# Token-major projection blocks as quads of 256 x 512 weight tiles in a hybrid decoder layer

## The chip, the cores and the metric

The kernel runs on one core of a Trainium2 chip. The metric is the device time of one execution in microseconds (us). Times of single instructions come from one profiled execution.

## What is computed

One decoder layer for 512 tokens of width 1024, batch 1, in float32. The normalised input goes through one combined projection, whose columns feed two mixers and two gates:

```python
h = rms_norm(x, norm1_w)
(q, k_c, v_c, k_s, v_s, k_w, v_w, g_nsa, z, xbc, dt_raw, gate_a, gate_b) = split_columns(h @ w_in, IN_SIZES)
y_a = nsa_mixer(...)      # 16 heads in 4 groups: compressed, selected and sliding-window attention
y_b = ssd_mixer(...)      # Mamba-2 scan, 32 heads in 4 groups, gated by silu(z), normalised per group
merged = sigmoid(gate_a) * (y_a @ w_proj_a) + sigmoid(gate_b) * (y_b @ w_proj_b)
x = x + merged @ w_out
x = x + conv_glu_ffn(rms_norm(x, norm2_w), ...)
```

## The kernel before, in words

**Split numbers.** Each product is made from three matmuls: high by high, high by low, low by high. A weight unit of 1024 x 128 is loaded by SyncE into one of two buffers `wraw` (two DMAs of 256 KB). ScalarE rounds it into `w_high` (`hi`, L1022, the activation is L1027), VectorE subtracts that and writes `w_low` (`lo`, L1548, the instruction L1551). Both have four slots. `load` for unit u waits until `lo(u - 2)` is done; `hi(u)` waits until TensorE is done with what lay in the slot. The activations lie transposed in `hT`, high and low.

**Phases.** 13 blocks come first (projections for the compressor and for group 0), then four groups g = 0 to 3 of 14 blocks each, then gates, the merge, the output projection and the feed-forward network. A block is one weight unit. The blocks of a group are OB, OC, then eight that are called windows n = 0 to 7 here, then four OX. Windows 0 to 3 (OQ) make queries, keys and values of the next group (in group 3: four gate blocks), windows 4 to 7 (OZ) make z of this group.

**Forms of a block.** `block_of` (through `gemm` and `ktile`, L609 to L611) holds a weight tile in the array and moves 512 tokens. `half_pair` (L637, matmuls L650 to L652) is token-major: it holds 128 x 128 tokens and moves the 256 columns of two neighbouring units; a pair of units takes two half_pairs, each of two token tiles, and each fills one of the two block banks `gb` (48 matmuls of 256 columns). It waits for both units of its pair.

**The interleave.** Every engine runs a list written out by hand. TensorE has eight places in a window, each of six matmuls of 256 columns (or three of 512). Between them it does, in window n: the scores of attention unit n + 1 (ahead of place 0), the weighted values of unit n - 1 (place 1), and the transposes of unit n's probabilities, j = 0, 1 at place 3 and j = 2, 3 at place 6 (window 0: places 2 and 5; window 7: 5 and 7). In window 0 of groups 1 to 3 the last y transposes stand at place 0. The transposes use two banks `tb` in turn, and each waits for the release (`t_rel`) of the one two before.

ScalarE, in stage n: `pT_hi` for j = 0, 1 (L1331), the exponentials of unit n + 1 for tiles 3 and 2 (L1294), `pT_hi` for j = 2, 3, the exponentials for tiles 1 and 0, the first convolution tap (L1101), and `evac_mid` (L1224), which copies the finished block out of its bank (for heads also a square for the norm) and ends with `hi(u + 3)`. In groups 1 to 3 it comes to stage 0 from `y_back_out` (L1183): four copies of y transposes into `ystage` (piece_e, L1189), each releasing a `tb` bank. `evac_x(g, 5)` (L1087), the evacuation of block OC with `hi` of unit OQ + 2, stands in stage 0 after the second `pT_hi`.

VectorE, in stage n:

```python
scale(n)                                  # L1835 to L1841, releases p_ready for the transposes of unit n
if n < 7: ttr(n + 1)                      # L1782, reads the scores, frees their banks
if n in (2, 4, 6): out_fold(n // 2 - 1)
lo(u0 + 4 + n)                            # unit OQ + 2 + n
p_low(n, ...)                             # L1853, releases the tb banks
if n > 1: conv(g, CONVS[n - 2])           # L1601
```

In stage 0 `comp_exponents` and `comp_probs`, in stage 1 `cmp_low`, in 5 `k_sums` and in 7 `q_sums` come besides. GpSimd does little in these windows.

## Time and profile before

| what | us |
|---|---|
| runs | 1243.45, 1243.58, 1244.14 |
| median | 1243.58 |
| profiled execution, span from first to last instruction | 1241.6 |
| TensorE busy | 1229.4 |
| VectorE busy | 843.6 |
| ScalarE busy | 635.3 |
| eight windows of group 1 (263.6 to 337.5) | 73.9 |

The span is from the first to the last instruction of the profiled execution. The profile gives no separate time for what lies outside the span; the median of the runs is 2.0 us above it. A matmul's length in the trace is modelled and overlaps the next one, so that the distance between starts tells what one costs. In a timeline row the columns are start, length, engine, line, operation, output<-inputs, shapes, count, and in brackets the idle time before it with its releaser.

### The profile page before, as it was taken

What the parts mean: (1) busy time and instruction counts of PE and PEld (TensorE: products, weight loads), DVE (VectorE), ACT (ScalarE), POOL (GpSimd) and SP (SyncE); (2) the same over time, 40 slices, a digit from 0 to 9 for tenths busy, and PEclk for the clock granted to TensorE, in tenths of its full rate; (3) what the DMA queues carried; (4) which work ended last, traced back from release to release, by engine and by line L of the source; (5) the groups of instructions that cost most, each with busy time, mean ns of one, the idle gap of its engine ahead of it and who ended that gap; (6) DMA issues with size and microseconds to landing.
All of it is one profiled execution on the core that took longest, in us unless ns stands there. A gap on an engine that the chain in (4) does not pass through costs nothing.

```text
span 1241.6 us, 17772 instructions
## 1 busy us (share of the span) xinstructions
PE 1229.4 (99%) x6725; PEld 1054.2 (85%) x6725; DVE 843.6 (68%) x1611; ACT 635.3 (51%) x1201; POOL 88.3 (7%) x78
## 2 busy tenths in 40 slices
PE   7999999999999999999999999999999999999998
PEld 6998998899978998888978888888888888888887
DVE  4526988898879887899774643333788888884221
ACT  6616777678775868676775633223423222332110
POOL 1000001400042001400040000000000000000000
PEclk9999999999999999999999999999999999999999
DMA  8512321132212221132116623335233333334341
GB/s 243 162 34 66 86 60 47 48 105 63 63 44 74 80 67 54 51 102 61 54 40 219 222 86 93 93 97 179 64 102 96 91 102 102 88 101 136 102 128 42
DMA packets 185737, 116.34 MB, mean 94 GB/s; under 512 B 25933, under 2 KB 169909, under 8 KB 185653
## 3 DMA queue, kind: packets, MB, share of 16 engines
q1 hardware_dynamic: 182023, 108.86, 30.5%
q10 hardware_dynamic: 3630, 6.35, 1.4%
q8 instruction: 54, 0.88, 0.3%
q14 instruction: 30, 0.25, 0.1%
HBM read 106.80 MB, written 8.39 MB: 93 GB/s over the span
## 4 chain that ended last, share of the span: by engine, by line
PE 94%; DVE 3%; ACT 1%; issue 1%; ACTq 0%; DVEq 0%
PE g L609 16%; PE g L611 16%; PE g L610 16%; PE t L602 5%; PE g L650 5%; PE g L652 5%; PE g L651 5%; PE ob L800 3%; PE s L784 3%; PE s L959 2%; PE s L960 2%; PE s L958 2%; PE t L706 1%; PE s L881 1%; PE g L959 1%; PE g L958 1%
## 5 line engine op out<-in xcount | busy, mean ns | idle before, releaser
L1027 ACT ACTIVATE w_high<-wraw 128x1024 fp32r<-128x1024 f32 x175 | 185.2, 1059 | 279.6 <-DMA wraw<-in_ffn_w_up 135.6
L1551 DVE TENSOR_TENSOR w_low<-wraw,w_high 128x1024 fp32r<-128x1024 f32 x174 | 216.7, 1248 | 125.7 <-ACT w_high L1027 123.2
L609 PE MATMUL g<-hT_hi,w_high 128*128 128x512 f32 x360 | 158.3, 440 | 1.2 <-DVE hT_lo L1557 1.2
L650 PE MATMUL g<-w_high,hT_hi 128*128 128x256 f32 x512 | 151.7, 296 | 0.2 <-DVE w_low L1551 0.2
L652 PE MATMUL g<-w_high,hT_lo 128*128 128x256 f32 x512 | 144.7, 283 | 0.0
L651 PE MATMUL g<-w_low,hT_hi 128*128 128x256 f32 x512 | 144.6, 282 | 0.0
L611 PE MATMUL g<-hT_hi,w_low 128*128 128x512 f32 x360 | 141.1, 392 | 0.0
L610 PE MATMUL g<-hT_lo,w_high 128*128 128x512 f32 x360 | 140.9, 391 | 0.0
L609 PE MATMUL g<-h2T_hi,w_high 128*128 128x512 f32 x352 | 137.4, 390 | 0.1
L610 PE MATMUL g<-h2T_lo,w_high 128*128 128x512 f32 x352 | 137.0, 389 | 0.0
L611 PE MATMUL g<-h2T_hi,w_low 128*128 128x512 f32 x352 | 137.0, 389 | 0.0
L650 PEld LDWEIGHTS g<-w_high,hT_hi 128*128 128x128 f32 x512 | 98.6, 193 | 0.7 <-issue 0.6
L651 PEld LDWEIGHTS g<-w_low,hT_hi 128*128 128x128 f32 x512 | 97.9, 191 | 0.5
L652 PEld LDWEIGHTS g<-w_high,hT_lo 128*128 128x128 f32 x512 | 97.5, 191 | 0.0
L609 PEld LDWEIGHTS g<-hT_hi,w_high 128*128 128x128 f32 x360 | 68.0, 189 | 17.0 <-issue 7.1
L610 PEld LDWEIGHTS g<-hT_lo,w_high 128*128 128x128 f32 x360 | 68.0, 189 | 15.8 <-issue 5.7
L611 PEld LDWEIGHTS g<-hT_hi,w_low 128*128 128x128 f32 x360 | 67.6, 188 | 15.2
L1331 ACT ACTIVATE pT_hi<-t 128x512 fp32r<-128x512 f32 (+3 forms) x128 | 49.3, 436 | 58.9 <-PE t L602 58.6
L609 PEld LDWEIGHTS g<-h2T_hi,w_high 128*128 128x128 f32 x352 | 66.1, 188 | 14.6 <-issue 0.7
L610 PEld LDWEIGHTS g<-h2T_lo,w_high 128*128 128x128 f32 x352 | 66.1, 188 | 13.6
L611 PEld LDWEIGHTS g<-h2T_hi,w_low 128*128 128x128 f32 x352 | 66.1, 188 | 13.6
L609 PE MATMUL g<-yT_hi,w_high 128*128 128x512 f32 x192 | 74.7, 389 | 0.0
(348 smaller groups left out, 2528.4 us busy)
## 6 DMA issues: line engine op xcount, KB each, us to landing
wraw<-in_w_in SPq DMA_DIRECT2D x152, 256.0 KB, 3.3
wraw<-in_ffn_w_up SPq DMA_DIRECT2D x88, 256.0 KB, 3.3
wraw<-in_ffn_w_down SPq DMA_DIRECT2D x44, 256.0 KB, 3.3
wraw<-in_w_proj_b SPq DMA_DIRECT2D x32, 256.0 KB, 3.2
yT_lo<-spill SPq DMA_DIRECT2D x6, 1024.0 KB, 10.4
spill<-piece_e ACTq DMA_DIRECT2D x16, 256.0 KB, 4.4
wraw<-in_w_proj_a SPq DMA_DIRECT2D x16, 256.0 KB, 3.2
wraw<-in_w_out SPq DMA_DIRECT2D x16, 256.0 KB, 3.3
```

The costliest lines, as they stand in the source:

```text
L602: last = nc.tensor.transpose(dst, src, ident[0:n, 0:n])
L609: nc.tensor.matmul(gb[par][:, :], w, hi, start=k == 0, stop=False)
L610: nc.tensor.matmul(gb[par][:, :], w, lo, start=False, stop=False)
L611: return nc.tensor.matmul(gb[par][:, :], wl, hi, start=False, stop=last)
L650: nc.tensor.matmul(out_, hT[0][:, k, cols], w, start=k == 0, stop=False)
L651: nc.tensor.matmul(out_, hT[0][:, k, cols], wl, start=False, stop=False)
L652: ins = nc.tensor.matmul(out_, hT[1][:, k, cols], w, start=False, stop=k == KD - 1)
L784: ins = nc.tensor.matmul(bk[:, o:o + w], qs[r][:, P * i:P * (i + 1)], k[:, 0:w], start=k is khh[br], stop=k is kll[br])
L800: ins = nc.tensor.matmul(ob[:, P * j:T], vst[:, br, j, :, :].rearrange("p a d -> p (a d)"), part[:, offT[j]:offT[j] + w], start=br == 0 an ...
L1027: nc.scalar.activation(whi[slot_of(u)][:, :, :], wraw[u % 2][:, :, :], ACT.Copy).then_inc(w_hi, 1)
L1331: nc.scalar.activation(pT[0][:, offT[j]:offT[j] + w], tb[par][:, 0:w], ACT.Copy).then_inc(pT_hi, 1)
L1551: V.tensor_tensor(wlo[slot_of(u)][:, :, :], wraw[u % 2][:, :, :], whi[slot_of(u)][:, :, :].bitcast(F32), ALU.subtract).then_inc(w_lo, 1)
```

## The change

Four neighbouring token-major units become a quad. Its weight tiles are 256 rows by 512 columns, one in each of the four slots, so that a matmul moves 512 columns. `quad_window` makes, in the first two of its four windows, token tiles 0 and 1 (first half of the 1024 rows, then second), each in one of the two block banks, and in the last two windows tiles 2 and 3. A window has 24 matmuls of 512 columns in eight places of three. Seven quads: heads and z in groups 0 to 2, z in group 3. The pairs at units 5 and 8 stay.

All four tiles are used until the end: the slots of the first two come free after the quad's third window (`quad_half`), of the others after the fourth. So `hi` and `lo` move: `hi` of OQ + 3, 5, 7, 9 to the middle of stages 0, 3, 4, 7 (behind the exponentials), of OQ + 4, 6, 8, 10 to the end of stages 2, 3, 6, 7; `lo` of OQ + 2, 4, 6, 8 to where `lo` was in stages 0, 3, 4, 7, and of OQ + 3, 5, 7, 9 to behind `p_low` of those stages, ahead of `conv`. The evacuations move to stages 1, 3, 5, 7: tile i = 0 of the pair behind `pT_hi` j = 1 and the exponentials there, i = 1 at the end. In groups 1 to 3 `evac_x(g, 5)` with its `hi` goes ahead of the fourth `ystage` copy. Heads tiles are loaded with three DMAs (256 rows of 256 query columns, and in each of these rows four pieces of 64 key and value columns), z tiles with two of 2 KB rows.

The diff, cut:

```diff
-PAIRS = {5, 8} | {U_GRP + GROUP_BLOCKS * g + o for g in range(G) for o in ((OQ, OQ + 2, OZ, OZ + 2) if g < G - 1 else (OZ, OZ + 2))}
+PAIRS = {5, 8}
+QUADS = [U_GRP + GROUP_BLOCKS * g + o for g in range(G) for o in (OQ, OZ) if g < G - 1 or o == OZ]
...
-def done_for_slot(u):
+def last_in_slot(u):
     before = [v for v in range(u) if slot_of(v) == slot_of(u)]
-    if not before:
-        return 0
-    return before[-1] + (2 if before[-1] in PAIRS else 1)
+    return before[-1] if before else None
+def loads_to(u):
+    heads = [first + q for first in QUADS if (first - U_GRP) % GROUP_BLOCKS == OQ for q in range(4)]
+    return sum(48 if v in heads else 32 for v in range(u % 2, u + 1, 2))
+def blocks_done(v):
+    for first in QUADS:
+        if first + 2 <= v < first + 4:
+            return first + 4
+    return v + (2 if v in PAIRS else 1)
+def quads_half_over(v):
+    for k, first in enumerate(QUADS):
+        if first <= v < first + 2:
+            return k + 1
+    return 0
...
+            def heads_rows(u, g, q):
+                rows = slice(2 * P * q, 2 * P * (q + 1))
+                dst = wide(wraw[u % 2])
+                qw = io["w_in"][0, rows, C_Q + 256 * g:C_Q + 256 * (g + 1)]
+                kv = io["w_in"][0, rows, C_KS:C_KS + 4 * 256].rearrange("(k p) (s n) -> p k s n", p=P, s=4)
+                load(u, [(dst[:, :, 0:256], qw.rearrange("(k p) n -> p k n", p=P))] + [
+                    (dst[:, kk, 256:512].rearrange("p (s n) -> p s n", s=4), kv[:, kk, :, DH * g:DH * (g + 1)])
+                    for kk in range(2)])
+            def z_rows(u, g, q):
+                wide_load(u, io["w_in"][0, :, C_Z + 512 * g:C_Z + 512 * (g + 1)], q, 0)
...
+            def quad_window(u, n, between):
+                first, tiles, half = u - n, (0, 1) if n < 2 else (2, 3), n % 2
+                place = 0
+                for i in tiles:
+                    if half == 0:
+                        pe.wait_ge(g_rel, first + i - 1)
+                    for q in (2 * half, 2 * half + 1):
+                        if i == 0:
+                            pe.wait_ge(w_lo, first + q + 1)
+                        w, wl = wide(whi[slot_of(first + q)]), wide(wlo[slot_of(first + q)])
+                        for kk in range(2):
+                            if place in between:
+                                between[place]()
+                            place += 1
+                            h, l = (t[:, 2 * q + kk, P * i:P * (i + 1)] for t in hT)
+                            out_ = gb[(first + i) % 2][:, :]
+                            nc.tensor.matmul(out_, h, w[:, kk, :], start=q == 0 and kk == 0, stop=False)
+                            nc.tensor.matmul(out_, h, wl[:, kk, :], start=False, stop=False)
+                            ins = nc.tensor.matmul(out_, l, w[:, kk, :], start=False, stop=q == 3 and kk == 1)
+                    if half == 1:
+                        ins.then_inc(mm_done, 1)
+                if n == 2:
+                    ins.then_inc(quad_half, 1)
...
-                    if u in PAIRS or u - 1 in PAIRS:
-                        half_pair(u, n % 2, between)
+                    if n >= 4 or g < G - 1:
+                        quad_window(u, n % 4, between)
...
             def hi(u):
-                if done_for_slot(u):
-                    act.wait_ge(mm_done, done_for_slot(u))
-                act.wait_ge(w_loaded[u % 2], 32 * (u // 2 + 1))
+                v = last_in_slot(u)
+                if v is not None:
+                    if quads_half_over(v):
+                        act.wait_ge(quad_half, quads_half_over(v))
+                    else:
+                        act.wait_ge(mm_done, blocks_done(v))
+                act.wait_ge(w_loaded[u % 2], loads_to(u))
...
-            def y_back_out(g):
+            def y_back_out(g, before_last=None):
                 act.wait_ge(t_rel, tau_of(g + 1, K_Y))
                 for b in range(4):
+                    if b == 3 and before_last:
+                        before_last()
...
+                ROUND_MID = {0: 3, 3: 5, 4: 7, 7: 9}
+                ROUND_END = {2: 4, 3: 6, 6: 8, 7: 10}
...
+                def evac_heads(i):
+                    u = u0 + OQ + i
                     act.wait_ge(mm_done, u + 1)
+                    src = gb[u % 2][:, :].rearrange("p (b n) -> p b n", b=4)
+                    nc.scalar.activation(tokq[:, :, i, :], src, ACT.Copy)
+                    nc.scalar.activation(sq[:, :, i, :], src[:, 0:2, :], ACT.Square)
+                    nc.scalar.activation(sq_k[:, :, i, :], src[:, 2:4, 0:DH], ACT.Square).then_inc(g_rel, 1)
+                def evac_z(c):
+                    u = u0 + OZ + c
+                    act.wait_ge(mm_done, u + 1)
+                    nc.scalar.activation(zs[:, c, :], gb[u % 2][:, :], ACT.Copy).then_inc(g_rel, 1)
...
                 if g:
                     y_scale(g - 1)
-                    y_back_out(g - 1)
+                    y_back_out(g - 1, lambda: evac_x(g, 5))
...
-                        if n == 0 and j == 1:
+                        if n == 0 and j == 1 and not g:
                             evac_x(g, 5)
+                        if n % 2 and j == 1:
+                            evac_tile(n, 0)
...
+                    if n in ROUND_MID:
+                        hi(u0 + OQ + ROUND_MID[n])
                     if n < 6:
                         first_tap(g, CONVS[n])
-                    evac_mid(n)
+                    if n < 4 and g == G - 1:
+                        evac_block(n)
+                    elif n % 2:
+                        evac_tile(n, 1)
+                    if n in ROUND_END:
+                        hi(u0 + OQ + ROUND_END[n])
...
-                    lo(u0 + 4 + n)
+                    for q in {0: (2,), 3: (4,), 4: (6,), 7: (8,)}.get(n, ()):
+                        lo(u0 + OQ + q)
...
                     if n == 7 and g < G - 1:
-                        dve.wait_ge(g_rel, u0 + OQ + 2)
+                        dve.wait_ge(g_rel, u0 + OQ + 4)
                         q_sums()
+                    for q in {0: (3,), 3: (5,), 4: (7,), 7: (9,)}.get(n, ()):
+                        lo(u0 + OQ + q)
                     if n > 1:
                         conv(g, CONVS[n - 2])
```


## Rows read from the trace of the kernel before

**Rows 1.** The page: its header and part 1, busy time, share of span, instructions.

```profile
span 1241.6 us, 17772 instructions
...
PE 1229.4 (99%) x6725; PEld 1054.2 (85%) x6725; DVE 843.6 (68%) x1611; ACT 635.3 (51%) x1201; POOL 88.3 (7%) x78
```

**Rows 2.** The page, part 4: the chain that ended last, by engine.

```profile
PE 94%; DVE 3%; ACT 1%; issue 1%; ACTq 0%; DVEq 0%
```

**Rows 3.** Stretches (columns: PE, PEld, DVE, ACT, POOL, clock, DMA): eight windows, groups 1, 0.

```profile
263.60:337.50 73.90, 73.74 (x577) 71.07 (x577) 64.71 (x175) 55.94 (x132) 0.00 (x0) 1.00 0.32 87
126.70:200.60 73.90, 73.65 (x571) 70.66 (x572) 64.81 (x175) 54.37 (x129) 0.00 (x0) 1.00 0.29 74
```

**Rows 4.** Groups of instructions by line and form, TensorE: busy us, mean ns.

```profile
L609 PE MATMUL g<-hT_hi,w_high 128*128 128x512 f32 x360 | 158.3, 440 | 1.2 <-DVE hT_lo L1557 1.2
L650 PE MATMUL g<-w_high,hT_hi 128*128 128x256 f32 x512 | 151.7, 296 | 0.2 <-DVE w_low L1551 0.2
```

**Rows 5.** Timeline, TensorE (start, length): two forms in group 1, down projection, start of window 0.

```profile
268.82 0.28 PE L652 MATMUL g<-w_high,hT_lo 128*128 128x256 f32 x1
...
270.61 0.28 PE L652 MATMUL g<-w_high,hT_lo 128*128 128x256 f32 x1
...
245.24 0.39 PE L610 MATMUL g<-hT_lo,w_high 128*128 128x512 f32 x1
...
246.85 0.39 PE L611 MATMUL g<-hT_hi,w_low 128*128 128x512 f32 x1
...
1200.20 0.39 PE L958 MATMUL g<-w_high,aT_hi 128*128 128x512 f32 x1
...
1202.92 0.39 PE L958 MATMUL t<-w_high,aT_hi 128*128 128x512 f32 x1
...
126.80 0.36 PE L650 MATMUL g<-w_high,hT_hi 128*128 128x256 f32 x1 [0.16 <-DVE w_low L1551]
```

**Rows 6.** Timeline, window 0 of group 1: ScalarE's fourth ystage copy, TensorE's transposes.

```profile
264.82 0.69 ACT L1189 ACTIVATE piece_e<-t,pcol 128x512 f32<-128x512 f32 x1 [0.49 <-ACT piece_e L1189]
...
265.33 0.93 PE L602 MATMUL t<-ident,piece_b 128*128 128x128 f32 x7
...
266.86 0.61 ACT L1093 ACTIVATE bcraw<-g 128x512 f32<-128x512 f32 x1
...
267.34 1.07 ACT L1027 ACTIVATE w_high<-wraw 128x1024 fp32r<-128x1024 f32 x1
```

**Rows 7.** Timeline, window 1 of group 1: VectorE's scale, TensorE's transposes.

```profile
273.59 1.27 DVE L1841 TENSOR_SCALAR piece_b<-piece_b,pscale 128x128 f32<-128x128 f32 x4
...
275.43 0.93 PE L602 MATMUL t<-ident,piece_b 128*128 128x128 f32 x7
```

**Rows 8.** Timeline, from window 3 to window 4 of group 1, three engines.

```profile
298.74 0.49 PE L602 MATMUL t<-ident,piece_b 128*128 128x128 f32 x3
...
299.16 0.55 ACT L1331 ACTIVATE pT_hi<-t 128x256 fp32r<-128x256 f32 x2 [0.43 <-PE t L602]
...
300.12 2.31 DVE L1601 SCALAR_TENSOR_TENSOR xcx<-xraw,pcol,xcx 128x511 f32<-128x511 f32 x3
...
300.48 0.81 ACT L1101 ACTIVATE xcx<-xraw,pcol 128x512 f32<-128x512 f32 x1
...
302.75 1.27 DVE L1841 TENSOR_SCALAR piece_b<-piece_b,pscale 128x128 f32<-128x128 f32 x4
...
305.44 0.93 PE L602 MATMUL t<-ident,piece_b 128*128 128x128 f32 x7
```

**Rows 9.** Timeline, second half of window 4 of group 1.

```profile
306.42 1.23 DVE L1551 TENSOR_TENSOR w_low<-wraw,w_high 128x1024 fp32r<-128x1024 f32 x1
...
307.68 1.15 DVE L1853 TENSOR_TENSOR pT_lo<-t,pT_hi 128x512 fp32r<-128x512 f32 x2
...
308.51 0.70 PE L602 MATMUL t<-ident,piece_b 128*128 128x128 f32 x3
```

**Rows 10.** The page, part 6: weight loads, KB each, median us to landing.

```profile
wraw<-in_w_in SPq DMA_DIRECT2D x152, 256.0 KB, 3.3
```

More of the change, by code:

```diff
@@ L263, in program @@
         w_hi, w_lo, mm_done, g_rel = sem("w_hi"), sem("w_lo"), sem("mm_done"), sem("g_rel")
+        quad_half = sem("quad_half")
         x_loaded = [sem(f"x_loaded{i}") for i in range(NT)]
@@ L424, in qkv, with wide_load @@
                 sides(u, w_in_cols(g * DH + k, DH), DH, w_in_cols(g * DH + v, DH), DH)
+            def wide_load(u, w, kq, h):
+                v = w[2 * P * kq:2 * P * (kq + 1), D // 2 * h:D // 2 * (h + 1)].rearrange("(k p) n -> p k n", p=P)
+                load(u, [(wide(wraw[u % 2])[:, kk, :], v[:, kk, :]) for kk in range(2)])
+            def heads_rows(u, g, q):
[8 more added lines that the diff above has]
+                wide_load(u, io["w_in"][0, :, C_Z + 512 * g:C_Z + 512 * (g + 1)], q, 0)
             def x_in(u, g, q):
@@ L446, in _ @@
                     if g < G - 1:
-                        qkv(u0 + OQ + b, g + 1, b)
+                        heads_rows(u0 + OQ + b, g + 1, b)
                     else:
@@ L450, in _ @@
                 for b in range(4):
-                    halves(u0 + OZ + b, w_in_cols(g * 512 + (C_Z + P * b)))
+                    z_rows(u0 + OZ + b, g, b)
                 for q in range(4):
@@ L480, in _ @@
                     halves(m * 3 + (U_MRG + q), w[:, m * P:(m + 1) * P])
-            def wide_load(u, w, kq, h):
-                v = w[2 * P * kq:2 * P * (kq + 1), D // 2 * h:D // 2 * (h + 1)].rearrange("(k p) n -> p k n", p=P)
-                load(u, [(wide(wraw[u % 2])[:, kk, :], v[:, kk, :]) for kk in range(2)])
             def out_unit(q):
@@ L1214, in evac_gate, with evac_tile, evac_block @@
                     hi(u + 3)
-                def evac_z(n):
-                    u, h, half = u0 + OQ + n, n % 2, n // 2 - 2
+                def evac_heads(i):
+                    u = u0 + OQ + i
                     act.wait_ge(mm_done, u + 1)
-                    nc.scalar.activation(zs[:, 2 * h:2 * h + 2, 256 * half:256 * (half + 1)],
-                                         gb[u % 2][:, :].rearrange("p (i n) -> p i n", i=2), ACT.Copy).then_inc(g_rel, 1)
-                    hi(u + 3)
-                def evac_mid(n):
+                    src = gb[u % 2][:, :].rearrange("p (b n) -> p b n", b=4)
[6 more added lines that the diff above has]
+                    nc.scalar.activation(zs[:, c, :], gb[u % 2][:, :], ACT.Copy).then_inc(g_rel, 1)
+                def evac_tile(n, i):
+                    if n >= 4:
+                        evac_z(2 * (n // 2 - 2) + i)
+                    elif g < G - 1:
+                        if n == 1 and i == 0:
+                            act.wait_ge(v_lo, g * 2 + 2)
+                        evac_heads(2 * (n // 2) + i)
+                def evac_block(n):
                     if n == 0:
                         act.wait_ge(v_lo, g * 2 + 2)
-                    if n >= 4:
-                        evac_z(n)
-                    elif g < G - 1:
-                        evac_tokens(u0 + OQ + n, n % 2, n >= 2)
-                    else:
-                        evac_gate(u0 + OQ + n, gate_tile(n))
+                    u = u0 + OQ + n
+                    act.wait_ge(mm_done, u + 1)
+                    nc.scalar.activation(gate_tile(n), gb[u % 2][:, :], ACT.Copy).then_inc(g_rel, 1)
                 def evac_late(q):
```

## The prediction

> **What bounds the kernel now.** I read the page's header first, then the chain that ended last, then the costliest groups, then stretches and single instructions of the second group. TensorE is busy in 99% of the span, VectorE in 68% [rows 1], and 94% of the chain is TensorE [rows 2]: whatever lengthens or interrupts TensorE's stream lengthens the run. But the change lies in eight windows of each of the four groups of heads, and there VectorE is not at 68%: in group 1 the eight windows take 73.9 us with VectorE busy for 64.71, in group 0 73.90 with 64.81 [rows 3], all at full clock. That leaves VectorE 9.2 us in eight windows, some 1.15 us in each, which is about the length of one low rounding of a weight tile (1.23 us [rows 9]). So TensorE ends last because VectorE just keeps up, and the question is what the change does to both.
>
> **TensorE, the 512-column form.** The trap is the mean duration. The 256-column matmuls show 296 ns, the 512-column ones of the same weights 440 [rows 4], and 7 quads of 192 short ones against 96 long ones would seem to give back 7 x (56.8 - 42.2) = 102 us. These durations overlap. The starts tell the price: 268.82 to 270.61 holds 15 steps of the 256-column form, 0.119 us each; 245.24 to 246.85 holds 7 steps of 512 columns in the same group phase, 0.230 each; 1200.20 to 1202.92 holds 12 steps of the very form that comes in (tokens stationary, 512 weight columns moving), 0.227 each [rows 5]. A window of 48 short matmuls costs 5.73 us, one of 24 long ones 5.52 (5.44 by the lower bound). I take 5.52, from the same phase of the kernel: 0.2 us a window. There are 28 such windows (8 in each of groups 0 to 2, 4 in group 3, which computes gates first): **-5.6 us**, bounds -5.6 and -8.1. Besides, the old form waits at window 0 for two rounded tiles, the new one for the first alone; in front of window 0 of group 0 TensorE waits 0.16 us for the second (126.80 [rows 5]), and groups 1 and 2 have the same order: **-0.5**.
>
> The Trainium skill ("TensorE: Matmul & The Clock Gate", Back-to-back issue gap) states N/2.4 + 2.5 ns for a warm gap. An estimate by that page is 5.24 against 5.18 us a window and a gain of 1.8 us, so that the sum below would come out 3.8 us higher; the starts in the rows are further apart than that for both forms, and the measurement decides.
>
> **What moves on VectorE and ScalarE.** The number of roundings stays. Their places change: a quad holds all four slots, so windows 1, 2, 5, 6 have no low rounding and 0, 3, 4, 7 have two, the second (of tiles OQ+3, +5, +7, +9) behind p_low and ahead of the convolution and of the next scale. Its ScalarE half comes only after the exponentials. The price is read where scale meets TensorE: p_transposes at place 3 of the next window.
>
> **(a) Window 0, groups 1 to 3: y_back_out.** TensorE transposes probabilities at 265.33 into a bank that ScalarE's fourth ystage copy frees; that copy starts at 264.82 [rows 6], so there is no slack. The change puts evac_x(g,5) and hi(OQ+2) ahead of it, which stood behind (266.86 and 267.34, 0.49 to the next start and 1.07 [rows 6]): 0.5 + 1.06, and the copy starts near 266.4 and frees the bank at 267.2, where TensorE stands at 265.5. **1.65 us x 3 = 5.0.** This needs tile OQ+2 to have landed by 265.4. Its loads are issued at about 261.4, and loads of w_in land after 3.3 us in the median [rows 10]; with 1,280 pieces in place of 2,048 I cost them at nothing, but a landing 1 to 2 us later adds as much to each of the two groups that load heads.
>
> **(b) Window 1.** Before, scale(1) starts its last part at 273.59 and ends at 274.86; TensorE comes at 275.43 [rows 7]: 0.5 us of slack. lo(OQ+3) now lies between, 1.14 us from start to start, and waits some 0.2 for its ScalarE half. Stall 0.9 in group 0; in the others, where (a) has held TensorE back, about 0.5: **2.4 in all**.
>
> **(c) Window 4, first half.** Window 3's second transposes start at 298.74; pT_hi j=2 follows at 299.16; the exponentials of the same stage are over when the first tap starts at 300.48; the convolution runs 300.12 to 302.35 and scale ends at 304.02, TensorE needs it at 305.44 [rows 8]. After: the evacuation of tile 2 stands ahead of pT_hi j=2: a copy of 512 columns (0.48, from 266.86 to 267.34 [rows 6]) and two squares of 256 and 128 columns, together about as much again, so 1.0, of which ScalarE's present wait takes up 0.3 and 0.7 delay it; exponentials to 301.2, hi(OQ+5) 1.06 to 302.25, lo(OQ+5) 1.24 to 303.5, convolution 2.23, scale 1.6: 307.3. TensorE, 0.2 earlier, waits **2.1 us**. In group 3 the windows 0 to 3 are gate blocks with no evacuation at that place: 1.3. Sum 3 x 2.1 + 1.3 = 7.6.
>
> **(d) Window 4, second half.** scale(4) is 3.3 us late (307.3 for 304.02), and behind it come ttr(5), the fold, lo(OQ+6) (306.42) and p_low(4) (307.68), on whose first two pieces the transposes at 308.51 depend; with 0.70 against 0.49 at 298.74 that row already shows 0.2 of wait [rows 9]. p_low moves to 311.0, its first two pieces end near 311.7 and 312.2, TensorE comes at 310.5 (308.51 + 2.1 - 0.1) and waits 1.3 for the first and 0.3 for the second, of which 0.2 were there before: **1.4 more than before, x 4 = 5.6.**
>
> **(e) Window 5.** lo(OQ+7) repeats (c) without an evacuation in its way: from the second transposes 0.42 + 1.32 + 1.06 + 1.24 + 2.23 + 1.6 = 7.9 us to the end of scale, where TensorE needs 6.7 less 0.3 (rows 298.74 to 305.44 [rows 8]): **1.4 x 4 = 5.6.** Windows 2, 3, 6 and 7 have no rounding ahead of their scale, and stall no more than now. Behind window 7 lo(OQ+9) leaves VectorE some 1.1 us later than TensorE's own shift; VectorE waits there for ScalarE's xcx copies before its second pair of products, which covers it. If not, 4 x 0.5 to 1 come on top.
>
> **Edits costed at nothing.** The extra squares on ScalarE (12 in place of 8 instructions a group) lie in its waits for TensorE, except in (c). The z loads become 2 KB pieces: the loads are issued two tiles ahead. A third DMA per heads tile lies on SP, which waits for w_low nearly throughout. The releases of the banks: tile 1's evacuation ends about 2 us before place 4 of window 2.
>
> **Sum.** Stalls 5.0 + 2.4 + 7.6 + 5.6 + 5.6 = 26.2, gains 6.1: **+20.1 us**. The stalls cannot be made good later, since TensorE has no other idle time to give. The profiled execution has a span of 1241.6 us [rows 1]; the median of the runs is 1243.58, 2.0 above it, and the same 2.0 is added. I say **1263**, a little below the sum since each stall uses slacks read to 0.1 or 0.2 us. Differences within 0.2% (2.5 us) of 1243.6 count as the same.
>
> **Rivals.** *The clumps are absorbed* (faster). VectorE's work per group is unchanged and it idles 9 us in the eight windows [rows 3]; if ScalarE's halves come earlier than I place them, lo alone (1.14) fits the slack of 1.4 in window 4, nothing follows in (d) and (e), and the fourth ystage copy makes do. Then only -6.1 is left: 1237.5. It needs (a) to vanish as well, against the zero slack in [rows 6]: 0.12. *Only (a) and (b) hold* and window 4 is absorbed: -6.1 + 7.4 = +1.3, 1245, the same: 0.08. *Slower than my sum*: late landing of the heads tiles (2 groups x 1 to 2 us in window 0), and VectorE's extra 1.1 us showing in the scan behind: 1267 to 1274: 0.15. My forecast with its own range 1254 to 1267 has 0.65. That the change doesn't do what it says is excluded for the matmul count, which is fixed by the loops.
>
> **Range.** 1245 to 1272: it takes in the case of no change and most of the high one, and leaves out the fast case and the far end of the high one, 0.15 together.
>
> **What would show it.** TensorE: 64 matmuls of 256 columns are left on each of the three lines (the two early pairs), and each of the three new lines has 224 of 512 columns, 0.23 us between starts. The waits of TensorE should now name VectorE: t <- piece_b (scale) in windows 1, 4 and 5, pT_lo in window 4, and piece_e of ScalarE in window 0 of groups 1 to 3. The eight windows should take 78 to 79 us in place of 73.9, in group 0 about 78. If they take 72, the first rival is right; if the waits of windows 4 and 5 are under 0.5 us each, step (c) was wrong and with it (d) and (e).

## The result and the profile after

The changed kernel takes **1268.29 us** (median of 4 runs, 1267.56 to 1269.63) against 1243.74 for the kernel before in the same comparison: ratio 1.02, 95% interval 1.0187 to 1.0214. The forecast was 1263, in a range of 1245 to 1272. The profiled execution has a span of 1266.1 us, 24.5 more than before. Two of the four executions show a mean granted clock of 0.998 and 0.999 and took 1268.8 and 1269.63 us; the two at 1.0 took 1267.56 and 1267.78.

The page of the changed kernel: header, busy times, and the chain that ended last (for [rows 1, 2]).

```profile
span 1266.1 us, 16431 instructions
...
PE 1226.2 (97%) x6053; PEld 1014.9 (80%) x6053; DVE 845.7 (67%) x1611; ACT 635.5 (50%) x1213; POOL 88.5 (7%) x78
...
PE 75%; DVE 14%; ACT 7%; issue 2%; DMA 1%; ACTq 0%; SPq 0%; DVEq 0%
```

TensorE has 672 matmuls fewer and is busy 3.2 us less, but the span has grown: its share falls from 99% to 97%. The chain says it more plainly. It ran through TensorE for 94% before, now for 75%, and crosses VectorE and ScalarE, which work no longer than before (845.7 for 843.6 us, 635.5 for 635.3). So the lost time is waiting, not work.

Groups by line and form of TensorE: the new form, and what is left of the old.

```profile
L705 PE MATMUL g<-w_high,hT_hi 128*128 128x512 f32 x224 | 95.1, 425 | 0.0
...
L706 PE MATMUL g<-w_low,hT_hi 128*128 128x512 f32 x224 | 87.7, 392 | 0.0
L683 PE MATMUL g<-w_high,hT_hi 128*128 128x256 f32 x64 | 18.3, 286 | 0.0
```

Counts are as the loops say. The mean of 392 to 425 ns beside a price of 0.23 us from start to start shows again that lengths of overlapping matmuls can't be summed.

What TensorE waited for in the changed kernel (line, releaser: us in total, times, longest).

```profile
PE t L635 <- DVE piece_b L1930: 13.6, 12, 1.7
PE t L635 <- DVE pT_lo L1942: 7.8, 8, 1.4
PE t L635 <- ACTq L1256: 5.4, 3, 2.1
PE g L748 <- POOL anyvis L585: 4.4, 1, 4.4
PE t L635 <- ACT sq L1458: 1.7, 4, 0.5
```

The fourth line, 4.4 us, was there before as 4.3. The others are the price: 28.5 us in 27 waits. Each is a transpose of TensorE. Those on `piece_b` and `pT_lo` wait for VectorE, and those on L1256 for ScalarE's `y_back_out` to free a bank. The timeline of group 1 places them; `piece_b` are the probabilities as `scale` leaves them, and a transpose of `cs` is one of the compressed attention.

```profile
272.88 0.55 PE L635 MATMUL t<-ident,piece_b 128*128 128x128 f32 x3 [2.05 <-ACTq L1256]
...
283.10 0.98 PE L635 MATMUL t<-ident,piece_b 128*128 128x128 f32 x7 [0.59 <-DVE piece_b L1930]
...
287.87 0.63 PE L635 MATMUL t<-ident,cs 128*128 128x128 f32 x4 [0.67 <-DVE pT_lo L1942]
...
314.30 0.98 PE L635 MATMUL t<-ident,piece_b 128*128 128x128 f32 x7 [1.65 <-DVE piece_b L1930]
...
318.74 0.70 PE L635 MATMUL t<-ident,piece_b 128*128 128x128 f32 x3 [1.40 <-DVE pT_lo L1942]
...
326.72 0.98 PE L635 MATMUL t<-ident,piece_b 128*128 128x128 f32 x7 [1.27 <-DVE piece_b L1930]
...
355.54 0.63 PE L635 MATMUL t<-ident,xcx 128*128 128x128 f32 x4 [0.46 <-ACT sq L1458]
```

In order: window 0, window 1 twice, window 4 twice, window 5, and one in the OX blocks. Two cases read on the other engines. Window 1, ScalarE in stage 1: the evacuation of token tile 0 (L1288 to L1290) is done first, and the second `pT_hi` behind it. The last row is another place, the high half of OQ + 5 in stage 3.

```profile
285.96 0.59 ACT L1288 ACTIVATE chan<-g 128x512 f32<-128x512 f32 x1
...
286.86 0.57 ACT L1411 ACTIVATE pT_hi<-t 128x256 fp32r<-128x256 f32 x2
...
308.07 1.09 ACT L1089 ACTIVATE w_high<-wraw 128x1024 fp32r<-128x1024 f32 x1
```

VectorE: the halves of `p_low` in stages 1 and 3, the low rounding of OQ + 5 behind stage 3 and the scale of window 4.

```profile
287.30 0.62 DVE L1942 TENSOR_TENSOR pT_lo<-t,pT_hi 128x256 fp32r<-128x256 f32 x2 [1.55 <-ACT pT_hi L1411]
...
307.21 0.62 DVE L1942 TENSOR_TENSOR pT_lo<-t,pT_hi 128x256 fp32r<-128x256 f32 x2 [1.36 <-ACT pT_hi L1411]
...
309.19 1.23 DVE L1640 TENSOR_TENSOR w_low<-wraw,w_high 128x1024 fp32r<-128x1024 f32 x1 [1.36 <-ACT w_high L1089]
...
312.97 1.27 DVE L1930 TENSOR_SCALAR piece_b<-piece_b,pscale 128x128 f32<-128x128 f32 x4
```

VectorE stands idle twice in stage 3, 1.36 us each: inside `p_low`, for ScalarE's second `pT_hi`, and ahead of the low rounding, for its high half (308.07). Then rounding, convolution and scale follow without a pause, and TensorE waits for the scale at 314.30.

Stretches of the changed kernel, from the first matmul of the first quad to the first of OX, in groups 0, 1 and 2 (columns as in [rows 3]):

```profile
126.34:205.46 79.12, 73.11 (x385) 59.50 (x383) 64.67 (x177) 53.92 (x134) 0.00 (x0) 1.00 0.22 62
268.76:349.06 80.30, 72.67 (x387) 59.88 (x385) 64.21 (x174) 55.37 (x136) 0.00 (x0) 1.00 0.24 73
412.38:492.80 80.42, 72.68 (x387) 59.88 (x385) 63.84 (x173) 55.38 (x136) 0.00 (x0) 1.00 0.24 71
```

The same stretches of the kernel before:

```profile
126.80:201.08 74.28, 74.12 (x576) 71.10 (x576) 65.07 (x175) 54.66 (x130) 0.00 (x0) 1.00 0.29 73
263.81:337.75 73.94, 73.78 (x578) 71.11 (x577) 64.78 (x174) 55.84 (x132) 0.00 (x0) 1.00 0.32 86
400.69:474.56 73.87, 73.53 (x579) 71.12 (x577) 64.49 (x173) 55.90 (x132) 0.00 (x0) 1.00 0.32 86
```

TensorE's busy time is 0.9 to 1.1 us lower in each, and they are 4.8, 6.4 and 6.6 us longer. Clocks are full in all six. From the same marks: window 0 of group 0 starts 0.46 earlier; windows 4 to 7 of group 3 take 39.52 for 36.03 (+3.5); from OX of group 2 to there +2.2; the OX blocks and what follows them in groups 0, 1 and 3 +0.57, +0.38, +0.55. Together 24.5, so everything is accounted for.

### The profile page after: what moved, and what is told of

The parts are those of the page before. It is cut to its first block, busy times and chain, and to the rows that moved or that the text cites. A ratio compares the mean times of both kernels' runs of the same rounds, so it can differ in the third digit from the quotient of the medians.

```text
span 1266.1 us, 16431 instructions
## 1 busy us (share of the span) xinstructions
PE 1226.2 (97%) x6053; PEld 1014.9 (80%) x6053; DVE 845.7 (67%) x1611; ACT 635.5 (50%) x1213; POOL 88.5 (7%) x78
## 4 chain that ended last, share of the span: by engine, by line
PE 75%; DVE 14%; ACT 7%; issue 2%; DMA 1%; ACTq 0%; SPq 0%; DVEq 0%
PE g L642 14%; PE g L644 14%; PE g L643 14%; PE t L635 3%; DVE w_low L1640 3%; PE g L705 2%; PE g L707 2%; PE g L706 2%; ACT piece_b L1374 2%; PE s L1017 2%; PE s L1018 2%; PE s L1016 2%; ACT w_high L1089 2%; PE ob L858 2%; PE s L842 1%
## 5 line engine op out<-in xcount | busy, mean ns | idle before, releaser
L705 PE MATMUL g<-w_high,hT_hi 128*128 128x512 f32 x224 | 95.1, 425 | 0.0
L707 PE MATMUL g<-w_high,hT_lo 128*128 128x512 f32 x224 | 88.3, 394 | 0.0
L706 PE MATMUL g<-w_low,hT_hi 128*128 128x512 f32 x224 | 87.7, 392 | 0.0
L1942 DVE TENSOR_TENSOR pT_lo<-t,pT_hi 128x512 fp32r<-128x512 f32 (+3 forms) x128 | 56.7, 485 | 39.9 <-ACT pT_hi L1411 39.8
L644 PEld LDWEIGHTS g<-hT_hi,w_low 128*128 128x128 f32 x360 | 67.6, 188 | 15.3
L643 PE MATMUL g<-yT_lo,w_high 128*128 128x512 f32 x192 | 74.7, 389 | 0.0
L644 PE MATMUL g<-yT_hi,w_low 128*128 128x512 f32 x192 | 74.7, 389 | 0.0
```

The lines of the kernel that those rows point to most:

```text
L643: nc.tensor.matmul(gb[par][:, :], w, lo, start=False, stop=False)
L644: return nc.tensor.matmul(gb[par][:, :], wl, hi, start=False, stop=last)
L705: nc.tensor.matmul(out_, h, w[:, kk, :], start=q == 0 and kk == 0, stop=False)
L706: nc.tensor.matmul(out_, h, wl[:, kk, :], start=False, stop=False)
L707: ins = nc.tensor.matmul(out_, l, w[:, kk, :], start=False, stop=q == 3 and kk == 1)
L1942: V.tensor_tensor(pT[1][:, offT[j]:offT[j] + w], tb[T_(K_UNIT[n] + j) % 2][:, 0:w], pT[0][:, offT[j]:offT[j] + w].bitcast(F32), ALU.subtra ...
```

## The experiments

Ten kernels were run. First theory: three clumps of work, each in a place where TensorE's next transposes hang on it: (A) the evacuation and rounding ahead of the fourth `ystage` copy; (B) roundings of OQ + 5 and OQ + 7 behind the exponentials and ahead of the convolution; (C) work on VectorE and ScalarE around the halves of `p_low` in window 1. The rival: the quads as such cost it, by the banks, the slots or the loads, and moving the clumps gives little. The kernel before was measured beside each set of runs, with medians of 1243.34 to 1243.74 us, so that a difference of two kernels from different sets is good to about 0.4 us. In the diffs of this section the line marks are left out.

**a_order0** undoes (A) alone.

```diff
                     y_scale(g - 1)
-                    y_back_out(g - 1, lambda: evac_x(g, 5))
+                    y_back_out(g - 1)
...
-                        if n == 0 and j == 1 and not g:
+                        if n == 0 and j == 1:
                             evac_x(g, 5)
```

> The kernel after, with evac_x(g, 5) and its hi back behind the second pT_hi of stage 0 in all groups. If the three waits of 2.05, 2.12 and 1.28 us on the ystage copy come from that order: they vanish, 1268.3 - 5.4 = 1263 (1262 to 1264). If they come from the late landing of the heads weights, the wait moves to hi(OQ+2) and the rounding of tile OQ+2 and at most 1.3 us is won in each heads group: 1265 to 1268. A new wait is possible at place 4 of window 0, where the bank of block OC is wanted: at most 0.3 us a group.

Measured 1262.42 us (1262.15 to 1262.55), ratio to before 1.0151 (1.0136 to 1.0166), 5.9 below the changed kernel, as expected. TensorE's waits: the line of L1256 is gone, and those on `piece_b` and `pT_lo` stand (the latter 7.8 us as before the edit).

```profile
PE t L635 <- DVE piece_b L1930: 13.5, 12, 1.7
```

The stretches of groups 1 and 2 fall from 80.30 and 80.42 to 78.48 and 78.31. So (A) holds, and is separate from the rest.

**b_order0** makes edit (A) alone in the kernel before, without any quad.

```diff
-            def y_back_out(g):
+            def y_back_out(g, before_last=None):
...
                 for b in range(4):
+                    if b == 3 and before_last:
+                        before_last()
...
-                    y_back_out(g - 1)
+                    y_back_out(g - 1, lambda: evac_x(g, 5))
...
-                        if n == 0 and j == 1:
+                        if n == 0 and j == 1 and not g:
```

> The kernel before with only evac_x(g, 5) and its hi moved ahead of the fourth ystage copy in groups 1 to 3. If that order alone costs what the traces of after say, without any quad: 1243.3 + 3 x 1.3 to 2.2 = 1247 to 1250. If the wait needs the quads or their loads: 1243 to 1244.

Measured 1249.32 us (1248.85 to 1250.7), 6.0 above before (1243.34 here), ratio 1.005 (1.0037 to 1.0064). The timeline shows the wait in group 1, at the transposes that stood at 265.33 without one [rows 6]:

```profile
268.13 0.55 PE L602 MATMUL t<-ident,piece_b 128*128 128x128 f32 x3 [2.19 <-ACTq L1194]
```

Three such waits make 4.7 us (2.19, 1.25 and 1.27), and the three windows 0 are longer by 2.33, 1.45 and 1.50 us: each wait costs about 0.2 more than the idle time shown for it. So the moved call costs about as much without the quads as with them. The wait in group 1 is the longest because ScalarE's rounding waits for its weights there too, although they come in the old way:

```profile
266.40 1.06 ACT L1027 ACTIVATE w_high<-wraw 128x1024 fp32r<-128x1024 f32 x1 [0.80 <-DMA wraw<-in_w_in]
```

**a_hi_only** leaves the evacuation ahead of the fourth copy and puts only the rounding of OQ + 2 back.

```diff
-                    y_back_out(g - 1, lambda: evac_x(g, 5))
+                    y_back_out(g - 1, lambda: evac_x(g, 5, following=False))
...
                             evac_x(g, 5)
+                        elif n == 0 and j == 1:
+                            hi(u0 + OQ + 2)
```

> The kernel after with the evacuation of block OC ahead of the fourth ystage copy, but hi(OQ+2) back behind the second pT_hi. Of the 1.28 us in group 3 and 2.05 to 2.12 in groups 1 and 2 the evacuation alone is worth 0.2 to 0.5 a group, the rounding with its wait for the load the rest: 1268.3 - 4.4 = 1264 (1263 to 1265). If the evacuation makes the wait: 1267 or more.

Measured 1263.3 us (1263.1 to 1263.61), ratio 1.0161 (1.0145 to 1.0176). The three waits on L1256 fall from 5.4 to 1.1 us in sum. Of 5.9 us the rounding is 5.0, the evacuation 0.9 (1263.3 against 1262.42). What the rounding does there is seen in ScalarE's timeline of the changed kernel, window 0 of group 1:

```profile
269.96 0.60 ACT L1155 ACTIVATE bcraw<-g 128x512 f32<-128x512 f32 x1 [0.55 <-ACT piece_e L1253]
...
271.14 1.06 ACT L1089 ACTIVATE w_high<-wraw 128x1024 fp32r<-128x1024 f32 x1 [0.58 <-DMA wraw<-in_w_in]
```

ScalarE is ready for the rounding 0.58 us before the weights have landed, in group 2 by 0.66, and only then follows the fourth copy at 272.11. In group 3, whose tile OQ + 2 is a gate block loaded as before, ScalarE doesn't wait for the load, and the wait of TensorE is 1.28 us against 2.05 and 2.12 in groups 1 and 2. That the heads tiles' form of load makes it late is not shown: b_order0 waits 0.80 us for an old load in group 1 and nothing in group 2.

**a_round** changes (B) alone. Both halves of each rounding are moved: ScalarE's to the end of stages 2 and 3, VectorE's to between the halves of `p_low`, where VectorE stood idle for 1.36 us.

```diff
-                ROUND_MID = {0: 3, 3: 5, 4: 7, 7: 9}
-                ROUND_END = {2: 4, 3: 6, 6: 8, 7: 10}
+                ROUND_MID = {0: (3,), 7: (9,)}
+                ROUND_END = {2: (4, 5), 3: (6, 7), 6: (8,), 7: (10,)}
...
-                    p_low(n, range(NT) if n else (2, 3))
+                    if n:
+                        p_low(n, (0, 1))
+                    for q in {3: (5,), 4: (7,)}.get(n, ()):
+                        lo(u0 + OQ + q)
+                    p_low(n, (2, 3))
...
-                    for q in {0: (3,), 3: (5,), 4: (7,), 7: (9,)}.get(n, ()):
+                    for q in {0: (3,), 7: (9,)}.get(n, ()):
```

> The kernel after, with hi(OQ+5) behind hi(OQ+4) at the end of stage 2, hi(OQ+7) behind hi(OQ+6) at the end of stage 3, and lo(OQ+5), lo(OQ+7) between the two halves of p_low of stages 3 and 4, where VectorE idles 0.6 to 1.3 us. If the place of the roundings costs the time (steps c, d, e), the waits of windows 4 and 5 (1.66 + 1.38 + 1.27 in a group, 17 in all) fall to under 0.5 a group: 1252 (1250 to 1255). If the quads themselves cost it (banks, slots held by a quad, evacuation in pairs), the waits stay and only change their releaser: 1264 or more.

Measured 1253.01 us (1252.09 to 1253.48), ratio 1.0077 (1.006 to 1.0094), 15.3 below the changed kernel. TensorE's waits:

```profile
PE t L635 <- ACTq L1256: 5.4, 3, 2.1
PE t L635 <- DVE pT_lo L1944: 4.7, 8, 0.7
...
PE t L635 <- DVE piece_b L1932: 2.0, 4, 0.6
```

VectorE's timeline of a_round in stage 3 of group 1, the moved rounding and the second half of `p_low`:

```profile
301.55 1.22 DVE L1642 TENSOR_TENSOR w_low<-wraw,w_high 128x1024 fp32r<-128x1024 f32 x1
302.99 0.62 DVE L1944 TENSOR_TENSOR pT_lo<-t,pT_hi 128x256 fp32r<-128x256 f32 x2 [0.23 <-ACT pT_hi L1411]
```

The rounding takes up the gap: of 1.36 us idle 0.23 are left. The eight waits for `scale` in windows 4 and 5 are gone, and the four left are window 1's. Window 4, from its scores to the next, takes 10.44 us where the changed kernel takes 13.0 and the kernel before 10.0; window 5 takes 9.2 for 10.9 and 9.43. Over the four groups these two windows give back 16.9 us. A lower clock in window 0 of group 2 (the last section) takes 1.3 of it again: 15.72 us for 14.16 in the changed kernel, with 0.3 less in window 1. The number of roundings is unchanged, and so are banks, slots and the form of the loads: the rival falls for these two windows.

**a_hi_early** keeps ScalarE's halves where a_round has them and puts VectorE's back behind `p_low`, to tell the two apart.

```diff
-                    for q in {3: (5,), 4: (7,)}.get(n, ()):
-                        lo(u0 + OQ + q)
...
-                    for q in {0: (3,), 7: (9,)}.get(n, ()):
+                    for q in {0: (3,), 3: (5,), 4: (7,), 7: (9,)}.get(n, ()):
```

(against a_round)

> The kernel after with hi(OQ+5) and hi(OQ+7) early as in a_round, but lo(OQ+5) and lo(OQ+7) where after has them, behind p_low and ahead of the convolution. If in steps (c) and (e) the wait of VectorE for ScalarE's half (about 1.5 us) is most of it and the 1.14 us of the low rounding fit the slack of 1.4 us: the waits on scale in windows 4 and 5 nearly vanish, within 2 us of a_round, 1253 to 1256. If the low rounding's own length costs it: 1258 to 1263, the waits fall by no more than a third.

Measured 1258.36 us (1256.21 to 1259.39), ratio 1.0113 (1.0098 to 1.0129). In the timeline of group 0, window 4:

```profile
169.03 0.98 PE L635 MATMUL t<-ident,piece_b 128*128 128x128 f32 x7 [0.21 <-DVE piece_b L1932]
...
173.47 0.70 PE L635 MATMUL t<-ident,piece_b 128*128 128x128 f32 x3 [1.39 <-DVE pT_lo L1944]
```

The wait for `scale` is down to 0.21 from 1.66, while that for `pT_lo` stays at 1.39. Window 4 takes 11.57 us against 13.05 in the changed kernel and 10.44 in a_round, window 5 takes 9.45 against 10.91 and 9.2. So in groups 0 to 2 ScalarE's place is worth 1.5 us in each of the two windows, VectorE's another 1.1 in window 4 and 0.25 in window 5. Group 3 is another case: window 4 takes 13.22 us there.

```profile
590.87 1.06 ACT L1089 ACTIVATE w_high<-wraw 128x1024 fp32r<-128x1024 f32 x1 [3.87 <-DMA wraw<-in_w_in]
...
595.40 0.70 PE L635 MATMUL t<-ident,piece_b 128*128 128x128 f32 x3 [2.79 <-DVE pT_lo L1944]
```

The load of OQ + 7 waits until `lo` of OQ + 5 is done. With that behind `p_low`, ScalarE's early rounding of OQ + 7 stands waiting for its weights, 1.6 us in groups 0 to 2 and 3.87 in group 3, where everything behind it on ScalarE is held back until TensorE waits. The result is neither of the two outcomes expected: the waits for `scale` nearly vanish, as the first says, but the time is that of the second. The wait for `pT_lo`, which neither had in it, stays, and three of the four executions show a mean clock of 0.997 to 0.999 and 1257.88 us or more; the one at 1.0 took 1256.21.

**a_comp** changes (C) alone: it moves `comp_probs` (2.0 us of VectorE) to between the halves of `p_low` in stage 1, and tile i = 0's evacuation behind the exponentials (stages 3, 5) or the last `pT_hi` (stage 1).

```diff
-                        if n % 2 and j == 1:
+                        if n == 7 and j == 1 or n == 1 and j == NT - 1:
                             evac_tile(n, 0)
...
+                    if n in (3, 5):
+                        evac_tile(n, 0)
...
-                    p_low(n, range(NT) if n else (2, 3))
-                    if n == 0:
+                    if n:
+                        p_low(n, (0, 1))
+                    if n == 1:
                         comp_probs()
+                    p_low(n, (2, 3))
```

> The kernel after, with comp_probs moved from stage 0 to between the halves of p_low of stage 1, and the evacuation of a pair's first tile moved behind the last pT_hi in stage 1 and behind the exponentials in stages 3 and 5. If window 1 loses its time to VectorE's lo(OQ+3) and to ScalarE's early evacuation (0.6 + 0.7 us a group), some 1.2 x 4 go, and another 0.4 to 0.7 in window 4: 1261.5 (1260 to 1264). If window 1 is bound by TensorE's own work, no change: 1268.

Measured 1272.94 us (1272.32 to 1273.92), ratio 1.0237 (1.0222 to 1.0252): 4.6 **slower** than the changed kernel where 6.8 faster was expected. TensorE's timeline, windows 1 and 4 of group 1:

```profile
284.96 0.98 PE L635 MATMUL t<-ident,piece_b 128*128 128x128 f32 x7 [0.34 <-DVE piece_b L1932]
...
290.10 0.63 PE L635 MATMUL t<-ident,cs 128*128 128x128 f32 x4 [1.04 <-DVE pT_lo L1944]
...
317.00 0.98 PE L635 MATMUL t<-ident,piece_b 128*128 128x128 f32 x7 [2.12 <-DVE piece_b L1932]
```

The wait for `pT_lo` grows by 0.37 (in group 3 by 0.8): 2.0 us of `comp_probs` do not fit where VectorE waits 1.55 (287.30 in the changed kernel). The wait for `scale` shrinks by 0.25 here and in group 2, but in groups 0 and 3 it stays at 0.63 and 0.56: it shrinks in the two groups whose window 0 ran in part at a lower clock, so that this isn't shown to be the edit's doing. In window 4 the evacuation now stands ahead of the rounding of OQ + 5, and the wait grows from 1.65 to 2.12. The larger part of the loss is the clock, told below: 3.5 us in window 0 of groups 1 and 2.

**a_all** is all three together.

> All three together. If the loss is order alone and the 512-column form gains 0.2 us a window as read from the starts: 1243.7 - 6 = 1238 (1236 to 1242), faster than both kernels. If the quads cost something of their own: 1246 or more. If the form gains more than the starts show (mean durations): under 1230.

Measured 1246.39 us (1246.17 to 1246.89, 10 runs), ratio 1.0024 (1.0014 to 1.0033), 8 above what was expected and, by its number alone, the outcome of the rival. Window 1 takes 11.4 to 12.0 us in groups 0 to 2, where the kernel before takes 10.2 to 10.3: the missing part, with waits of 1.0 to 1.1 for `pT_lo` and of 0.3 to 0.7 for `scale`. The next two kernels take the two waits apart.

**a_three** is a_all with `comp_probs` back in stage 0.

```diff
-                    if n == 1:
-                        comp_probs()
                     p_low(n, (2, 3))
+                    if n == 0:
+                        comp_probs()
```

> As a_all, but with comp_probs back in stage 0. a_all kept a loss of 1.7 us in each window 1 against the kernel before (0.63 on scale behind lo(OQ+3), 1.03 on p_low behind comp_probs). If moving comp_probs was the wrong step, the second of these waits goes and the first stays: 1246.4 - 4 = 1242.4 (1241.5 to 1243.5). If it makes no difference (TensorE waits as long for something else): 1246.

Measured 1243.03 us (1242.73 to 1243.99, 11 runs), ratio 0.9998 (0.9989 to 1.0007): 3.4 less than a_all, by the place of `comp_probs` alone. The later evacuation has no run of its own, but seems to help: the changes of a_order0 and a_round together would give 1268.3 - 5.9 - 15.3 = 1247.1, and this kernel is 4.1 below that. Of that 1.3 is a_round's window with a lower clock, and windows 1 and 4 are shorter than a_round's by 2.0 in sum over the groups: the wait of the compressed transposes falls from 0.7 to 0.2 us in groups 0 to 2, and that for `pT_lo` in window 4 from 0.7 to 0.4. The rest is not placed. TensorE's waits:

```profile
PE t L635 <- DVE pT_lo L1946: 2.5, 8, 0.5
...
PE t L635 <- DVE piece_b L1934: 2.2, 4, 0.6
```

**a_best** takes the last four `piece_b` waits away. In the second window of a quad the weight halves go outside and the token tiles inside, so that tile OQ + 3 is wanted at place 4 in place of place 2, and its low rounding moves from ahead of `scale(1)` to behind it.

```diff
-                for i in tiles:
-                    if half == 0:
+                qs_ = (2 * half, 2 * half + 1)
+                turns = [(i, q) for q in qs_ for i in tiles] if n == 1 else [(i, q) for i in tiles for q in qs_]
+                for i, q in turns:
+                    if half == 0 and q == 0:
...
-                    if half == 1:
+                    if half == 1 and q == 3:
                         ins.then_inc(mm_done, 1)
...
                     scale(n)
+                    if n == 1:
+                        lo(u0 + OQ + 3)
...
-                    for q in {0: (3,), 7: (9,)}.get(n, ()):
+                    for q in {7: (9,)}.get(n, ()):
```

> As a_three, and in the second window of a quad the halves of the weight rows are the outer loop and the two token tiles the inner one, so that tile OQ+3 is wanted at place 4 and not at place 2, and lo(OQ+3) goes behind scale(1). If the wait in window 1 is lo(OQ+3) ahead of scale(1): another 0.6 x 4 go, 1240 (1238.5 to 1241.5), faster than the kernel before by what the 512-column form gains. If the four slots make a wait somewhere in window 1 in any case: 1242 or more.

Measured **1240.33 us** (1239.76 to 1240.82, 11 runs), ratio to before **0.9976 (0.9967 to 0.9984)**: the quads in another order beat both kernels, by 3.0 us and 28. The waits of a_best, and the same three stretches:

```profile
PE t L635 <- ACT sq L1464: 1.7, 4, 0.5
PE t L635 <- DVE pT_lo L1948: 1.6, 5, 0.4
```

```profile
126.50:199.72 73.22, 72.37 (x385) 59.83 (x383) 64.18 (x177) 54.03 (x134) 0.00 (x0) 1.00 0.24 68
263.00:335.64 72.64, 72.22 (x387) 60.07 (x385) 63.64 (x174) 55.35 (x136) 0.00 (x0) 1.00 0.27 80
398.90:471.62 72.72, 71.86 (x386) 60.16 (x385) 63.40 (x173) 55.30 (x136) 0.00 (x0) 1.00 0.27 78
```

VectorE does as much as in the changed kernel (63.64 for 64.21) in 7.7 us less. The longest wait left among these is 0.5 us.

Not all of the 3.0 us is the 512-column form. Window 2, from scores to scores, takes 9.41 to 9.44 us for 10.12 and 10.13 in groups 0 to 2, and 9.41 for 9.99 in group 3, where windows 0 to 3 are gate blocks of the same form in both kernels. What goes there is a short stall of the kernel before, at the second transposes, behind a low rounding that window 2 no longer has:

```profile
562.15 0.70 PE L602 MATMUL t<-ident,piece_b 128*128 128x128 f32 x3 [0.21 <-DVE pT_lo L1853]
```

It is worth some 0.5 us a group beyond the 0.2 of the form, 2.1 us in sum. Whether the kernel before would gain it by moving that rounding, without quads, was not run.

**a_best_silu** tries the wait of 0.46 us in OX, at the transposes of the xcx copies: the rounding of OQ + 10, which ScalarE does at the end of stage 7 ahead of them, goes between the second and the third of the copies.

```diff
-                ROUND_END = {2: (4, 5), 3: (6, 7), 6: (8,), 7: (10,)}
+                ROUND_END = {2: (4, 5), 3: (6, 7), 6: (8,)}
...
+                    if c == 2:
+                        hi(u0 + OQ + 10)
                     t_wait(tau)
```

> a_best, and hi(OQ+10) moved from the end of stage 7 to between the second and third of ScalarE's copies after the x transposes, where it idles for TensorE. If the wait of 0.47 us in block OX of each group comes from ScalarE carrying one more rounding at the end of stage 7: 1240.3 - 1.8 = 1238.5 (1238 to 1239.5). If it comes from the SiLU pieces or the banks: 1240.

Measured 1240.04 us (1239.88 to 1240.44, 7 runs), ratio 0.9972 (0.9961 to 0.9983): not told from a_best. Three of the four waits stand (1.4 us in sum), so that rounding is not their cause. What is was not found: neither the place of `lo` of OQ + 9 nor that of the copies was tried.

## Why the prediction was right, and where it was off

The sign, the mechanism and the places were right. The sum was +20.1, the spans say +24.5. The measured 1268.3 lies inside the stated range, but outside the 1254 to 1267 that had 0.65, in the band of the third rival, which had 0.15; and the eight windows take 79.1, 80.3 and 80.4 us for 78 to 79 forecast. Two sums of the prediction are slightly off: step (e) comes to 7.9 - 6.4 = 1.5 and not 1.4, and the estimate by the page to a gain of 1.7 and not 1.8.

**The form** was right, and so was taking it from starts: windows without a wait in either kernel are 0.2 shorter (window 3: 9.18 for 9.37; window 5 of a_best: 9.20 for 9.43). The missed gain is window 2, 0.7 shorter in the changed kernel already. The start of group 0's windows, 0.46 earlier, is the half microsecond counted for the second rounded tile. The back-to-back rule weighed in the prediction (the Trainium skill, "TensorE: Matmul & The Clock Gate", Back-to-back issue gap), which that section gives for an isolated matmul, would have allowed 0.06 us a window, an estimate; the 0.2 of windows 3 and 5 are against it here.

**(a)** was forecast at 1.65 x 3 = 5.0, and two experiments give 5.9 and 6.0. In group 3 the wait is 1.28. In groups 1 and 2 it is 2.05 and 2.12, of which 0.58 and 0.66 are the landing of the weights, counted there as nothing and named as a risk of 1 to 2 us; the rest, some 1.5, is a little under the 1.65. In the sum this term is short by about 0.9. That the kernel before with the one edit loses as much (b_order0) shows that the zero slack read in [rows 6] was a true reading.

**(b)** was right in size for the scale of window 1 (0.59 for 0.5 in group 1), but missed the wait of the compressed transposes in the same window, 0.67, behind `p_low` of halves 2 and 3, which the earlier evacuation holds back on ScalarE. a_three bears the reason out: with the evacuation behind that `pT_hi`, 0.2 of the 0.7 is left. Window 1 is longer by 1.3, 1.0 and 1.1 us in groups 0 to 2 for 0.7 and twice 0.3 forecast. Window 2, which has no rounding any more, is 0.7 shorter for 0.2 forecast, and this hides some two thirds of the miss. Windows 1 and 2 together are longer by 0.6, 0.3 and 0.4 in groups 0 to 2 for 0.5, 0.1 and 0.1.

**(c), (d), (e)**, the largest terms, held: 1.65, 1.40 and 1.27 us of wait in group 1 for 2.1, 1.4 and 1.4. Windows 4 and 5 are longer by 3.05 and 1.48, or 4.5 together, as forecast (4.9 less two gains of 0.2). a_round takes 15.3 us away by moving two roundings a group, 16.9 in these windows alone; the three terms were 18.8, and its window 4 still stands 0.45 above before. a_hi_early then says why (c) comes about, in the way the step put it: with ScalarE's half early, VectorE's 1.24 us fit the slack ahead of `scale` but for 0.2. As to (d), the run shows what the step's arithmetic says when the lateness changes: its wait is how late VectorE's line is less how late TensorE is. In the forecast that was 3.3 less 2.1. Counted from the window's scores, `scale` in group 1 ends 3.1 us later than before in the changed kernel, where TensorE has been held 1.65; in a_hi_early it ends 1.6 later, and TensorE has been held 0.2. Both leave 1.4 to 1.5, and the waits are 1.40 and 1.36. So a mended (c) does not mend (d). Only a rounding put where VectorE had waited does (a_round, 0.7 at most).

**The edits costed at nothing** are where the rest went. "VectorE waits there for ScalarE's xcx copies ... which covers it. If not, 4 x 0.5 to 1 come on top": a wait of 0.46 is there in all four groups, +1.5 in sum over the OX blocks of groups 0, 1 and 3. The mechanism given is not shown, since the wait names ScalarE, and the one rounding tried, ScalarE's of OQ + 10, was not its cause; `lo` of OQ + 9 was not moved. The extra 4.4 us are thus about 1.5 in OX, 2.7 in the stretches of groups 0 to 2, and 0.2 in group 3. Of the 2.7, window 0 has 1.8, of which 0.9 is (a), and windows 1 and 2 have 0.6.

**The rivals.** *The clumps are absorbed* said 1237.5. It was wrong for the changed kernel, but near to right on its condition: with the roundings in VectorE's gaps, the evacuations later and the fourth copy left alone the kernel comes to 1243.03, and with window 1 mended as well to 1240.33. So quads and new order together are worth 3.0 us here, half of the 6.1 counted for the quads, although some 2 us of window 2's stall went besides. Against them stand the waits that remain (`pT_lo` 1.6 and OX 1.7 in sum, each costing somewhat more than its idle time). *Late landing* was real at 0.6 us in two groups, below the 1 to 2 given.

## What to carry to other kernels

An engine off the chain with 12% of slack, as VectorE had here, has that slack spread in pieces; a change that keeps its work but puts two pieces of it together can cost more than the change gains: between the changed kernel and a_best, the same quads in another order, lie 28 us. So place work into the gaps where the engine waits today. If it needs a first half from another engine, move both halves, since here the two places were worth 1.5 and up to 1.1 us a window, and moving the first alone made it wait up to 3.87 us for its weights, whose load hung on the second half of an earlier tile. Read the length of a gap before you fill it: 1.22 us went into one of 1.36, while 2.0 us did not and cost 3.4 us in four groups.

## What the hardware showed that was not expected

TensorE's granted clock fell behind some waits of 2 us and stayed at full behind others of the same length. In a_comp's window 0 of group 1, after the wait of 2.05 us that ends at 273.42 (the one that the changed kernel has at 272.88), stretches of 2 us show (the granted clock is the third column from the end):

```profile
274.00:276.00 2.00, 2.00 (x6) 1.53 (x6) 1.50 (x3) 0.78 (x2) 0.00 (x0) 0.50 0.38 140
276.00:278.00 2.00, 2.00 (x9) 1.60 (x8) 1.97 (x3) 0.13 (x1) 0.00 (x0) 0.68 0.00 0
```

The same place in the changed kernel:

```profile
274.00:276.00 2.00, 2.00 (x12) 1.65 (x11) 1.97 (x4) 0.47 (x2) 0.00 (x0) 1.00 0.20 78
```

At 0.50, which is the 1.2 GHz level, six matmuls stand in 2 us for twelve in the changed kernel, with starts 0.43 us apart in place of 0.23 at 2.4 GHz. Window 0 of that group took 15.61 us for 14.08 in the changed kernel, so a drop costs some 1.5 us behind a wait of 2. It came too in a_comp's group 2 behind a wait of 2.58 us (0.50 from 421 to 423), in a_round (group 2, behind 2.09 us, 0.57 and 0.58 from 408 to 412) and in a_hi_early behind a wait of 2.79 us (0.64 and 0.51 from 596 to 600). But behind a wait of 2.43 us in a_hi_early (group 2, ending at 410.56) the clock is 1.00 to 416. What decides whether it comes after such a wait is open: the length of the wait alone does not, and no run was made for it. It means that a wait of 2 us can cost 3.5, and that a_comp's time says less about its edits than its waits do: in its profiled execution window 0 of groups 1 and 2 alone took 1.5 and 2.0 us more than in the changed kernel, and all four of its executions show a mean clock of 0.995 or 0.996.
